# Tile norms, section sums, layer 1's scores and the first routing of a two-layer decoder trunk in another order, on one core

## The chip, the core and the metric

The kernel runs on one core of a Trainium2 chip. The metric is the device time of one execution in microseconds (us). The version before takes 1516.17 us in the median of three runs (1515.65 to 1516.95).

## What is computed

The reference is a two-layer decoder trunk on 256 tokens of width 1024, float32 in and out. Each layer turns a conditioning vector into six sections of 1024 values (shift, scale and gate of the mixer, then of the feed-forward part), normalizes the rows, runs a hybrid mixer, and adds a feed-forward part: a dense SwiGLU in layer 0, the top two of eight experts in layer 1.

```
mod = (silu(c) @ ada_w[l] + ada_b[l])          # sections 6l .. 6l+5: sh1, sc1, g1, sh2, sc2, g2
h = rmsnorm(x, norm_mix_w[l]) * (1 + sc1) + sh1
x = x + g1 * hybrid_mixer(h, ...)              # conv | HGRN2 recurrence | chunked gMLP, then @ w_o
h = rmsnorm(x, norm_ffn_w[l]) * (1 + sc2) + sh2
ffn = swiglu(h, w1, w3, w2)                    if l == 0
ffn = sum of gates[e] * swiglu_e(h), e in top-2 of softmax(h @ router_w + router_b)   if l == 1
x = x + g2 * ffn
out = rmsnorm(x, final_norm_w)
```

The recurrence of the HGRN2 branch is computed here as masked scores on nine levels (block sizes 1, 2, 4, ... 128 tokens), each a set of small matmuls whose result Vector keeps under a mask.

## The kernel before

The tokens are two tiles of 128 (tt = 0 and 1). The weights, 474 MB in all, are loaded once in pieces of 128x1024 into a ring of 11 buffers (`raw`). ScalarE copies each piece rounded (its high part), Vector subtracts to get the low part (`split`, a ring of six), and TensorE multiplies in three passes (high by high, low by high, high by low). `s_lo` counts the low parts, `s_used` the pieces that TensorE is done with. Each engine's program is written out by hand in order, and semaphores join them. PSUM has two rings with an order fixed by tables: single banks `psU` (`unit_plan`) and pairs of banks `psA` (`event_plan`); `open_unit` and `open_event` wait until the bank's last reader is done.

Four places matter here.

**Tile norms.** The last product before a norm (w_o in a mixer, w2 in the dense part) ends with four held pieces, so that tile 0 is complete before tile 1. In `norm_tiles` Vector adds each half row to the residual (`add_rows`), ScalarE squares (`tile_square`) and takes the root (`tile_root`), Vector scales the rows (`tile_rows`), TensorE transposes the tile (`turn_tile`), and ScalarE scales and shifts the eight transposed chunks out of PSUM (`tile_high`, one activation for each) and writes them in pairs, rounded, to `hS`. Vector subtracts for the low part (`tile_low`). Then `rows_by_tiles` multiplies the next weight: three pieces on tile 0, the transposes of tile 1, the fourth piece, and then four pieces on tile 1. n = 0 is the norm before the dense part, n = 1 that before layer 1's mixer, n = 2 the router's.

**Section sums.** Vector accumulates a section's product with the conditioning vector over eight pieces (`product`), and TensorE sums over the partitions against a column of ones: `ada_sum` makes eight columns of one PSUM bank, which `modulate` reads; `row_sum` makes a row. Sections 3 and 4 of layer 0 feed n = 0, sections 7 and 6 feed n = 1. Section 11 is summed too at the end of the dense part.

**Scores.** `level` makes the scores of one level on TensorE, `keep_scores` keeps them, `prepare` makes the next level's operands. `sgu_mix` (spatial gating) takes the next pair of banks after level 8, and so waits until level 7's scores are kept; `attend` waits for level 8's.

**Routing.** `logits` of both tiles, Vector's top two, a rank of each token among those of its expert (a matmul with a triangle of ones), a selection matrix, and `gather`, which multiplies the tokens by it. Then a loop over the experts' items begins; it takes half of the time.

## Time and profile before

| | |
|---|---|
| median of three runs | 1516.17 us |
| the profiled execution, its own time | 1515.74 us |
| span of its trace | 1513.9 us |
| TensorE busy | 1484.2 us (98%) |
| TensorE weight loads | 1260.1 us (83%) |
| Vector busy | 1300.1 us (86%) |
| ScalarE busy | 961.2 us (63%) |
| mean granted TensorE clock | 0.993 |

The time of an execution is the span plus about 1.8 us around it. Busy time of TensorE (PE) counts pipelined matmuls; PEld is its weight loads, DVE is Vector, ACT is ScalarE. A float32 matmul that isn't in the rounded format stands in the trace as two records: `ada_sum` has 8 matmuls and 16 records. The granted clock is 1.00 at 2.4 GHz and 0.50 at 1.2 GHz.

### The profile page before, as it was taken

The numbers are of one execution on the slowest core, as the hardware profiler recorded it, in microseconds if no ns is written. First come the engines' busy times: TensorE is split into PE (matmuls) and PEld (weight loads), VectorE is DVE, ScalarE is ACT, GpSimd is POOL, SyncE is SP. The second block draws the span as 40 slices with busy tenths as digits, with TensorE's granted clock in tenths as the row PEclk, the third lists the DMA queues.
The fourth block names the chain that finished last, engine by engine and source line by source line (L and its number), as shares of the span: only waits on it lengthen the run. The fifth ranks groups of instructions, "written<-read, shape, count | busy, mean of one in ns | idle before, by whom it ended". The sixth has DMA issues, their size and how long they took to land. (4 is left out here: it accounts for less than half of the span.)

```text
span 1513.9 us, 22427 instructions
## 1 busy us (share of the span) xinstructions
PE 1484.2 (98%) x7543; PEld 1260.1 (83%) x7543; DVE 1300.1 (86%) x1508; ACT 961.2 (63%) x1120; POOL 30.0 (2%) x50
## 2 busy tenths in 40 slices
PE   8999999999999999999899999999999999999997
PEld 7999888788887998888788888888888888888886
DVE  7999797687665798797799999999999999999998
ACT  3636445644435544444397887887878878788785
POOL 0000000000000000000010000000000000000100
PEclk9999999999999999999899999999999999999999
DMA  9956497599994745588299999999999999999993
GB/s 349 342 172 237 142 336 273 177 342 352 354 328 144 250 140 195 208 313 291 92 363 396 410 393 400 380 370 411 359 390 379 375 409 360 395 369 384 410 393 138
DMA packets 196979, 473.91 MB, mean 313 GB/s; under 512 B 16252, under 2 KB 64564, under 8 KB 196916
## 3 DMA queue, kind: packets, MB, share of 16 engines
q1 hardware_dynamic: 192288, 457.27, 82.1%
q0 software_dynamic: 4352, 15.73, 2.7%
q8 instruction: 36, 0.59, 0.2%
q14 instruction: 27, 0.22, 0.0%
q10 hardware_dynamic: 276, 0.09, 0.0%
HBM read 457.83 MB, written 15.21 MB: 312 GB/s over the span
## 5 line engine op out<-in xcount | busy, mean ns | idle before, releaser
L1339 ACT ACTIVATE split<-raw 128x1024 fp32r<-128x1024 f32 x750 | 780.5, 1061 | 281.7 <-PE psU L731 169.7
L2257 DVE TENSOR_TENSOR split<-raw,split 128x1024 fp32r<-128x1024 f32 x528 | 617.1, 1222 | 22.8 <-ACT split L1339 10.5
L731 PE MATMUL psU<-split,yS 128*128 128x512 f32 x2448 | 565.2, 390 | 0.2 <-DVE split L2257 0.2
L731 PEld LDWEIGHTS psU<-split,yS 128*128 128x128 f32 x2448 | 457.9, 188 | 95.3 <-DVE split L2257 0.8
L731 PE MATMUL psU<-split,hS 128*128 128x512 f32 (+1 forms) x1488 | 340.7, 387 | 1.4 <-DVE hS L1839 1.3
L731 PEld LDWEIGHTS psU<-split,hS 128*128 128x128 f32 x1488 | 273.4, 190 | 58.8 <-issue 5.1
L1656 DVE TENSOR_TENSOR split<-raw,split 128x1024 fp32r<-128x1024 f32 x222 | 264.1, 1219 | 42.8 <-ACT split L1339 41.9
L731 PE MATMUL psA<-split,hidE 128*128 128x512 f32 x1056 | 246.0, 392 | 0.0
L731 PEld LDWEIGHTS psA<-split,hidE 128*128 128x128 f32 x1056 | 196.5, 188 | 40.1
L731 PE MATMUL psU<-hS,split 128*128 128x256 f32 x1248 | 155.2, 285 | 0.1
L731 PEld LDWEIGHTS psU<-hS,split 128*128 128x128 f32 x1248 | 151.3, 192 | 1.3 <-issue 1.2
L1515 ACT ACTIVATE sig<-psU 128x512 f32<-128x512 f32 x24 | 13.0, 596 | 73.4 <-PE psU L731 73.4
L731 PE MATMUL psA<-split,hid_hi 128*128 128x512 f32 x176 | 55.2, 395 | 0.0
L1742 DVE SCALAR_TENSOR_TENSOR adacc<-raw,cact,adacc 128x1024 f32<-128x1024 f32 x42 | 53.8, 1281 | 1.1
L2438 DVE TENSOR_TENSOR hidE<-psA,hidE 128x512 fp32r<-128x512 f32 (+1 forms) x48 | 29.5, 643 | 14.4 <-ACT hidE L1339 14.4
L731 PEld LDWEIGHTS psA<-split,hid_hi 128*128 128x128 f32 x176 | 32.6, 188 | 6.9 <-issue 0.5
L1339 ACT ACTIVATE hidE<-psA 128x512 fp32r<-128x512 f32 (+1 forms) x48 | 25.3, 560 | 18.6 <-PE psA L1238 18.6
L2431 DVE TENSOR_TENSOR sig<-sig,psU 128x512 f32<-128x512 f32 (+1 forms) x48 | 29.3, 639 | 6.6 <-PE psU L731 6.6
L1597 ACT ACTIVATE sig<-psU 128x512 f32<-128x512 f32 (+1 forms) x48 | 25.3, 562 | 4.1 <-PE psU L731 4.1
L1339 ACT ACTIVATE work<-psU 128x512 f32<-128x512 f32 x18 | 10.4, 598 | 25.4 <-PE psU L731 20.6
L731 PE MATMUL psA<-split,hid 128*128 128x512 f32 x64 | 25.0, 390 | 0.0
L1238 PEld LDWEIGHTS psA<-ident,sig 128*128 128x128 f32 x176 | 21.3, 141 | 4.2
(287 smaller groups left out, 814.0 us busy)
## 6 DMA issues: line engine op xcount, KB each, us to landing
raw<-in_moe_w_dram SPq DMA_DIRECT2D x496, 512.0 KB, 5.9
raw<-in_w_in_dram SPq DMA_DIRECT2D x116, 512.0 KB, 6.0
raw<-in_ada_w_dram SPq DMA_DIRECT2D x96, 512.0 KB, 6.7
raw<-in_ffn_w_dram SPq DMA_DIRECT2D x66, 512.0 KB, 7.3
raw<-in_moe_w_dram SPq DMA_DIRECT2D x64, 256.0 KB, 6.2
raw<-in_w_o_dram SPq DMA_DIRECT2D x16, 512.0 KB, 5.9
token_rows<-sc SPq DMA_DIRECT2D x11, 512.0 KB, 10.7
raw<-in_w_br_a_dram SPq DMA_DIRECT2D x8, 512.0 KB, 6.7
```

What stands on the lines that cost most here:

```text
L731: return pe.matmul(o, a, b, start=start, stop=stop, skip_group_check=True)
L1238: last = pe.transpose(T_BANKS[g % 2][:, m * CAP:(m + 1) * CAP], sig[0:CAP, 2 + g % 2, m * P:(m + 1) * P], ident[0:CAP, 0:CAP])
L1339: return act.activation(o, i, ACT.Copy)
L1515: act.activation(sig[:, j, :], bank[:, :], ACT.Sigmoid).then_inc(s_uA, 1)
L1597: act.activation(sig[0:CAP, g % 2, 0:width], psU[3 if g == MIXED else g % 2][0:CAP, 0:width], ACT.Silu).then_inc(s_silu, 1)
L1656: TTN(split[:, n % SPL, 1, :], raw[:, SPLIT_POS[n] % RAW, :], split[:, n % SPL, 0, :].bitcast(F32), ALU.subtract).then_inc(s_lo, 1)
L1742: STT(acc, raw[:, pos % RAW, :], cact[:, k:k + 1], acc, ALU.mult, ALU.add).then_inc(s_afree, 1)
L2257: TTN(split[:, slot, 1, :], raw[:, (RAW0 + n) % RAW, :], split[:, slot, 0, :].bitcast(F32), ALU.subtract).then_inc(s_lo, 1)
L2431: TTN(sig[0:CAP, 2 + g % 2, 0:width], s, three, ALU.mult).then_inc(s_hrow, 1)
L2438: TTN(h_lo, T_BANKS[g % 2][:, 0:len(tiles) * CAP], h_hi.bitcast(F32), ALU.subtract).then_inc(s_hlo, 1)
```

## The change

- The three sums of `NORM_SUMS` (7, 6 and 11) no longer stand among the pieces of w2 but together between tile 0's and tile 1's held pieces. The sums of sections 3 and 4 in layer 0 stand between the two tiles' held pieces of w_o. Each of these sums now has 64 equal columns in place of one, eight times 64 filling a bank, of which `modulate` reads one.
- `turn_tile` of tile 0 comes two pieces earlier at n = 0, and one half row earlier at n = 1.
- In `tile_high` a chunk's activation no longer waits for the one before it; the copy of a pair comes one chunk late and waits only for its own two chunks.
- Vector's order in `norm_tiles` follows, with single chunk pairs between the residual's half rows.
- In layer 1 `keep_scores` of level 7 and the low parts of the next two pieces come before the last tap of the convolution.
- Tile 0 is ranked, selected and gathered on its own, while tile 1's logits and top two are made. The filling matmuls ahead of it are 2, not 4.

The diff, cut to its core:

```diff
-ROW_SUMS = [2, 5, 8, 9, 10]
...
-DOWN_SUM_AT = {2: 7, 3: 6, BANKWISE - 1: 11}
...
-FILL_LOGITS = 4
+FILL_LOGITS = 2
...
-        plan += [(("ada", 6 * l + s), "D") for s in (2, 3)]
-        plan += [((l, "merge", i), "merged") for i in range(2)] + [(("ada", 6 * l + 4), "D")]
+        plan += [(("ada", 6 * l + s), "D") for s in ((2, 3) if l else (2,))]
+        plan += [((l, "merge", i), "merged") for i in range(2)]
+        plan += [(("ada", 6 * l + s), "D") for s in ((4,) if l else (3, 4))]
...
-                    last = mm(bank[:, k:k + 1], acc[:, k * P:(k + 1) * P], ones[:, 0:1], True, True)
+                    last = mm(bank[:, k * WIDE:(k + 1) * WIDE], acc[:, k * P:(k + 1) * P], ones[:, 0:WIDE], True, True)
...
-            def section_sum(s):
-                row_sum(s) if s in ROW_SUMS else ada_sum(s)
...
-                        if (n, hh) == (2, 0):
-                            section_sum(6 * l + 3)
+                        if (l, n, hh) == (1, 2, 0):
+                            row_sum(9)
...
                         banks = [open_unit((l, "y" + b, 2 * hh + tt)) for tt in range(TT)]
...
-                        section_sum(6 * l + 2)
+                        row_sum(6 * l + 2)
...
                     if n == 1:
...
-                section_sum(6 * l + 4)
+                if l:
+                    row_sum(10)
                 for hh, q in WO_PIECES[HELD:]:
                     pe.wait_ge(s_ml, 4 * l + q + 1)
                     ws.append(next_split())
...
+                if l == 0:
+                    ada_sum(3)
+                    ada_sum(4)
...
                     rows_piece(wo[hh], q, ws[n], 1).then_inc(s_used, 1)
-                    if n == 2:
+                    if n == 2 * l:
...
-                    elif f in DOWN_SUM_AT:
-                        ada_sum(DOWN_SUM_AT[f])
...
-                                if f == NF - 2:
-                                    turn_tile(1, 0)
...
+                        if (tt, hh) == (0, 1):
+                            for s in NORM_SUMS:
+                                ada_sum(s)
+                        if (tt, hh) == (1, 0):
+                            turn_tile(1, 0)
...
-            def logits(tt):
...
-                for k in range(KD):
+            def logits(tt, ks=range(KD)):
...
+                for k in ks:
...
-                last.then_inc(s_unit, 1)
+                if ks[-1] == KD - 1:
+                    last.then_inc(s_unit, 1)
...
-            logits(1)
-            bank = open_unit("rank")
+            logits(1, range(4))
+            rank = open_unit("rank")
...
-            mm(bank[:, 0:NE], tri[:, :], route[:, 0, 0:NE], True, True)
-            mm(bank[:, NE:3 * NE], ones[:, :], route[:, 0:1, 0:NE].to_broadcast([P, 2, NE]), True, False)
-            mm(bank[:, NE:2 * NE], tri[:, :], route[:, 0, NE:2 * NE], False, True)
-            mm(bank[:, 2 * NE:3 * NE], ones[:, :], route[:, 0, NE:2 * NE], False, True).then_inc(s_unit, 1)
...
-            def gather(banks):
...
-                for m in range(KD):
-                    for tt in range(TT):
-                        last = mm(banks[m // 4][:, (m % 4) * CAP:(m % 4 + 1) * CAP], htok[:, tt, m * P:(m + 1) * P],
-                                  sel[:, 0, tt, :], tt == 0, tt == 1)
-                    if m % 4 == 3:
+            mm(rank[:, 0:NE], tri[:, :], route[:, 0, 0:NE], True, True)
+            mm(rank[:, NE:3 * NE], ones[:, :], route[:, 0:1, 0:NE].to_broadcast([P, 2, NE]), True, False).then_inc(s_rank, 1)
+            logits(1, range(4, KD))
...
+            def gather(banks, tt, ms):
...
+                pe.wait_ge(s_sel, tt + 1)
+                for m in ms:
+                    last = mm(banks[m // 4][:, (m % 4) * CAP:(m % 4 + 1) * CAP], htok[:, tt, m * P:(m + 1) * P],
+                              sel[:, 0, tt, :], tt == 0 and m % 4 == 0, tt == 1)
+                    if tt and m % 4 == 3:
...
-            pe.wait_ge(s_sel, 1)
-            gather(open_event("gather0"))
+            banks = open_event("gather0")
+            gather(banks, 0, range(6))
+            pe.wait_ge(s_rt, 2)
+            mm(rank[:, NE:2 * NE], tri[:, :], route[:, 0, NE:2 * NE], False, True)
+            mm(rank[:, 2 * NE:3 * NE], ones[:, :], route[:, 0, NE:2 * NE], False, True).then_inc(s_unit, 1)
+            gather(banks, 0, range(6, KD))
+            gather(banks, 1, range(KD))
...
+                first = step[0]
...
+                def pair_high(j):
+                    if j < 3:
+                        act.wait_ge(s_a, first + 2 * j + 2)
+                    else:
+                        act.wait_ge(s_eA, emptied(EVENTS, at, "A"))
+                    copy(hS[:, 0, 2 * j:2 * j + 2, tt * P:(tt + 1) * P],
+                         xn[tt][:, 2 * j * P:2 * (j + 1) * P].rearrange("p (a b) -> p a b", a=2)).then_inc(s_th, 1)
...
-                        act.wait_ge(s_eA, emptied(EVENTS, at, "A"))
...
-                        link(ins)
-                    if k % 2:
-                        copy(hS[:, 0, k - 1:k + 1, tt * P:(tt + 1) * P],
-                             xn[tt][:, (k - 1) * P:(k + 1) * P].rearrange("p (a b) -> p a b", a=2)).then_inc(s_th, 1)
+                        ins.then_inc(s_a, 1)
+                        step[0] += 1
+                    if k % 2 == 0 and k:
+                        pair_high(k // 2 - 1)
+                pair_high(3)
...
                 tile_root(n, 0)
+                if n == 0:
+                    high_parts(held + 7)
+                tile_high(n, 0)
...
-                tile_high(n, 0)
...
-                TTN(dst, bank[:, 0:KD], vecs[:, ADA_B + 8 * s:ADA_B + 8 * s + 8],
+                TTN(dst, bank[:, :].rearrange("p (k r) -> p k r", r=WIDE)[:, :, 0], vecs[:, ADA_B + 8 * s:ADA_B + 8 * s + 8],
...
                 tile_base(n, 0)
+                if n:
+                    modulate(7)
+                    modulate(6)
...
+                for s in ((11,) if n else (3, 4)):
+                    modulate(s)
+                if n == 0:
+                    low_parts(held + 7)
+                tile_low(n, 0, range(1))
...
+                tile_low(n, 0, range(1, 3))
+                add_rows(n, 1, 1, row)
+                tile_low(n, 0, range(3, 4))
...
-                tile_low(n, 0, range(2))
-                add_rows(n, 1, 1, row)
-                tile_low(n, 0, range(2, 4))
...
                 keep_scores(l, 6)
                 prepare(l, 8)
                 lows_beside((l, "i", 1))
+                if l:
+                    keep_scores(l, 7)
+                    lows_beside((l, "u", 0))
...
-                    elif j:
-                        lows_beside((l, "u", 0))
-                    keep_scores(l, 7 + j)
+                    if j or l == 0:
+                        keep_scores(l, 7 + j)
...
-                            else:
-                                modulate(3)
...
-                    modulate(4)
...
-                if f in (6, 7):
-                    modulate(NORM_SUMS[f - 6])
...
-            modulate(DOWN_ADA[0])
...
+                of = slice(tt * NE, (tt + 1) * NE)
...
-                TTN(route[:, LG, tt * NE:(tt + 1) * NE], bank[:, 0:NE], rtb[:, :], ALU.add).then_inc(s_uD, 1)
+                TTN(route[:, LG, of], bank[:, 0:NE], rtb[:, :], ALU.add).then_inc(s_uD, 1)
...
-                link(dve.max(mx8[:, tt, :], route[:, LG, tt * NE:(tt + 1) * NE]))
-                settle()
-                link(dve.max_index(ix8[:, tt, :], mx8[:, tt, :], route[:, LG, tt * NE:(tt + 1) * NE]))
-                settle()
-                link(dve.tensor_copy(route[:, IDX, tt * NE:(tt + 1) * NE], ix8[:, tt, :]))
+                link(dve.max(mx8[:, tt, :], route[:, LG, of]))
+                settle()
+                link(dve.max_index(ix8[:, tt, :], mx8[:, tt, :], route[:, LG, of]))
+                settle()
+                link(dve.tensor_copy(route[:, IDX, of], ix8[:, tt, :]))
...
-                    link(TS(route[:, row, tt * NE:(tt + 1) * NE], iota8,
-                            route[:, IDX, tt * NE + k:tt * NE + k + 1], None, ALU.is_equal))
-            TTN(cur[:, 0:2], mx8[:, :, 0], mx8[:, :, 1], ALU.subtract).then_inc(s_prob, 1)
-            settle()
-            TTN(route[:, SEL, :], route[:, ONE, :], route[:, TWO, :], ALU.add).then_inc(s_rt, 1)
-            dve.wait_ge(s_rt, 1)
-            bank = unit("rank")
-            link(TTN(route[:, POS, :], bank[:, 0:2 * NE], route[:, SEL, :], ALU.mult))
-            dve.tensor_copy(route[:, CNT, 0:NE], bank[:, 2 * NE:3 * NE]).then_inc(s_uD, 1)
-            settle()
-            for tt in range(TT):
+                    link(TS(route[:, row, of], iota8, route[:, IDX, tt * NE + k:tt * NE + k + 1], None, ALU.is_equal))
+                settle()
+                TTN(route[:, SEL, of], route[:, ONE, of], route[:, TWO, of], ALU.add).then_inc(s_rt, 1)
+                dve.wait_ge(s_rt, tt + 1)
+                if tt:
+                    bank = ready("rank")
+                else:
+                    dve.wait_ge(s_rank, 1)
+                    bank = psU[UNIT_AT["rank"] % 4]
+                link(TTN(route[:, POS, of], bank[:, of], route[:, SEL, of], ALU.mult))
+                settle()
...
-                ins = TS(sel[:, 0, tt, :], slots[:, :], route[:, POS, tt * NE:tt * NE + 1], None, ALU.is_equal)
-                if tt == 0:
-                    link(ins)
-            ins.then_inc(s_sel, 1)
+                TS(sel[:, 0, tt, :], slots[:, :], route[:, POS, tt * NE:tt * NE + 1], None, ALU.is_equal).then_inc(s_sel, 1)
+            dve.tensor_copy(route[:, CNT, 0:NE], bank[:, 2 * NE:3 * NE]).then_inc(s_uD, 1)
+            TTN(cur[:, 0:2], mx8[:, :, 0], mx8[:, :, 1], ALU.subtract).then_inc(s_prob, 1)
...
```

The order of instructions, with the wait of each in brackets. First TensorE's program at n = 0, in layer 0's w_o and the dense part's first pieces (`psU<-split,hS` are the pieces, `psA<-ident,merged` the transposes of a tile, `psA<-ones,...` the section sums), as a piece of the difference:

```order
 L837 MATMUL psA<-ident,merged 128x128 x8
-L731 MATMUL psU<-split,hS 128x512 x24
-L731 MATMUL psA<-ones,work 128x1 x8
-L731 MATMUL psU<-split,hS 128x512 x42
+L731 MATMUL psU<-split,hS 128x512 x48
+L731 MATMUL psA<-ones,adacc 128x64 x8
+L731 MATMUL psA<-ones,work 128x64 x8
+L731 MATMUL psU<-split,hS 128x512 x6
 L799 MATMUL psA<-ident,merged 128x128 x8
-L731 MATMUL psU<-split,hS 128x512 x24
+L731 MATMUL psU<-split,hS 128x512 x36
 L799 MATMUL psA<-ident,merged 128x128 x8
```

Both sums now stand between the 24 held matmuls of tile 0 and those of tile 1, and tile 0's transposes have three held pieces and three pieces of tile 0 behind them where they had one and three.

Vector's program in layer 1 around the last scores, before (`sc<-...` keeps scores, `split` rows make low parts, `work<-work,vecs` is the tap, `work<-psA,vecs,sgub` reads the spatial gating):

```order
L1955 TENSOR_TENSOR work<-work 128x4x128
L2078 SCALAR_TENSOR_TENSOR work<-work,vecs 128x254 [waits dve_step]
L2078 SCALAR_TENSOR_TENSOR work<-work,vecs 128x254 x3
L2091 TENSOR_TENSOR work<-work 128x1024 [waits dve_step]
L1996 COPY_PREDICATED sc<-masks,psA 128x512 [waits dve_event_emptied,event_ready]
L1996 COPY_PREDICATED sc<-masks_back,psA 128x4x128
L1656 TENSOR_TENSOR split<-raw,split 128x1024 [waits act_high_parts] x2
L1992 COPY sc<-psA 128x512 [waits dve_event_emptied,event_ready]
```

and now:

```order
L1981 TENSOR_TENSOR work<-work 128x4x128
L2022 COPY_PREDICATED sc<-masks,psA 128x512 [waits dve_event_emptied,event_ready]
L2022 COPY_PREDICATED sc<-masks_back,psA 128x4x128
L1674 TENSOR_TENSOR split<-raw,split 128x1024 [waits act_high_parts] x2
L2104 SCALAR_TENSOR_TENSOR work<-work,vecs 128x254 [waits dve_step]
L2104 SCALAR_TENSOR_TENSOR work<-work,vecs 128x254 x3
L2120 TENSOR_TENSOR work<-work 128x1024 [waits dve_step]
L2018 COPY sc<-psA 128x512 [waits dve_event_emptied,event_ready]
```

The level-7 scores and the two low parts moved ahead of the five instructions of the convolution.

TensorE's program from the second logits to the gather, before (`rtw,merged` logits, `route` the rank, `sc,work` the gather):

```order
L731 MATMUL psU<-rtw,merged 128x64 [waits router_first_chunks_ready]
L731 MATMUL psU<-rtw,merged 128x64 x3
L731 MATMUL psU<-rtw,merged 128x64 [waits act_event_emptied]
L731 MATMUL psU<-rtw,merged 128x64 x3
L731 MATMUL psU<-route,tri 128x8 [waits routing_ready,dve_unit_emptied]
L731 MATMUL psU<-route,ones 128x16
L731 MATMUL psU<-route,tri 128x8
L731 MATMUL psU<-route,ones 128x8
L731 MATMUL psA<-sc,work 128x128 [waits act_event_emptied,selection_ready]
L731 MATMUL psA<-sc,work 128x128 x15
```

and now:

```order
L731 MATMUL psU<-rtw,merged 128x64 x3
L731 MATMUL psU<-route,tri 128x8 [waits selected_experts_ready,dve_unit_emptied]
L731 MATMUL psU<-route,ones 128x16
L731 MATMUL psU<-rtw,merged 128x64 [waits act_event_emptied]
L731 MATMUL psU<-rtw,merged 128x64 x3
L731 MATMUL psA<-sc,work 128x128 [waits selection_ready,act_event_emptied]
L731 MATMUL psA<-sc,work 128x128 x5
L731 MATMUL psU<-route,tri 128x8 [waits selected_experts_ready]
L731 MATMUL psU<-route,ones 128x8
L731 MATMUL psA<-sc,work 128x128 [waits selection_ready]
L731 MATMUL psA<-sc,work 128x128
L731 MATMUL psA<-sc,work 128x128 [waits selection_ready]
```

Tile 0's rank stands between two halves of the logits, and half of the gather no longer waits for tile 1.

## Rows read from the trace of the kernel before

**Rows 1.** The page's first part, busy time of TensorE: us, share, instructions.
```profile
PE 1484.2 (98%) x7543; PEld 1260.1 (83%) x7543; DVE 1300.1 (86%) x1508; ACT 961.2 (63%) x1120; POOL 30.0 (2%) x50
```
**Rows 2.** Waits of TensorE, longest first: us in total, times, longest.
```profile
PE psA L799 <- DVE split L1656: 5.1, 2, 2.5
...
PE psA L731 <- DVE sc L1996: 3.0, 1, 3.0
```
**Rows 3.** Windows of TensorE: length, PE busy and count, granted clock, DMA.
```profile
283.80:287.20 3.40, 3.15 (x12) 0.54 0.53 152
484.90:488.30 3.40, 3.40 (x10) 0.50 0.51 155
580.70:584.00 3.30, 3.30 (x18) 0.51 0.00 0
734.00:737.50 3.50, 3.10 (x12) 0.51 0.00 0
747.80:754.70 6.90, 6.05 (x29) 0.51 0.01 2
```
**Rows 4.** Timeline, n = 0: start, length, engine, line, count, [idle before].
```profile
264.53 9.84 PE L731 MATMUL psU<-split,hS 128*128 128x512 f32 x42
...
280.10 0.61 ACT L1385 ACTIVATE sig<-xs 128x512 f32<-128x512 f32 x1
...
282.77 1.22 DVE L1656 TENSOR_TENSOR split<-raw,split 128x1024 fp32r<-128x1024 f32 x1
...
284.05 1.97 PE L799 MATMUL psA<-ident,merged 128*128 128x128 f32 x8 [2.54 <-DVE split L1656]
```
**Rows 5.** Timeline, n = 1, TensorE.
```profile
463.67 0.72 PE L731 MATMUL psA<-split,hid_hi 128*128 128x512 f32 x2
...
476.74 4.58 PE L731 MATMUL psU<-split,hS 128*128 128x512 f32 x18 [0.98 <-DVE hS L1839]
...
483.86 1.09 PE L799 MATMUL psA<-ident,merged 128*128 128x128 f32 x8 [2.55 <-DVE split L1656]
...
484.71 8.68 PE L731 MATMUL psU<-split,hS 128*128 128x512 f32 x30
```
**Rows 6.** Timeline, layer 1's last scores.
```profile
576.04 1.65 DVE L2078 SCALAR_TENSOR_TENSOR work<-work,vecs 128x254 f32<-128x254 f32 x4
...
577.72 1.23 DVE L2091 TENSOR_TENSOR work<-work 128x1024 f32<-128x1024 f32 x1
...
580.32 3.60 PE L731 MATMUL psA<-wT,merged 128*128 128x128 f32 x16 [3.00 <-DVE sc L1996]
...
601.40 3.35 DVE L2139 RECIPROCAL work<-work 128x512 f32<-128x512 f32 x1 [1.82 <-ACT work L1357]
```
**Rows 7.** Timeline, routing.
```profile
745.83 0.17 DVE L2304 TENSOR_TENSOR route<-psU,rtb 128x8 f32<-128x8 f32 x1 [1.94 <-PE psU L731]
...
747.44 0.36 PE L731 MATMUL psU<-route,tri 128*128 128x8 f32 x2 [1.64 <-DVE route L2317]
...
749.85 6.07 PE L731 MATMUL psA<-sc,work 128*128 128x128 f32 x32 [0.85 <-DVE sc L2326]
...
755.68 14.63 PE L731 MATMUL psU<-split,yS 128*128 128x512 f32 x63
```
**Rows 8.** Timeline: a one-column sum, 64-column logits, small matmuls at 1.00.
```profile
461.97 1.84 PE L731 MATMUL psU<-ones,adacc 128*128 128x1 f32 x16
...
589.57 2.84 PE L731 MATMUL psA<-sc,work 128*128 128x128 f32 x24
...
738.17 1.89 PE L731 MATMUL psU<-rtw,merged 128*128 128x64 f32 x16
```
**Rows 9.** Timeline, ScalarE, the first chunks of tile 0 at n = 0.
```profile
274.92 0.95 ACT L1410 ACTIVATE merged<-psA,mod,wm 128x128 f32<-128x128 f32 x2 [1.15 <-PE psA L799]
...
275.90 0.42 ACT L1339 ACTIVATE hS<-merged 128x256 fp32r<-128x256 f32 x1
...
276.23 0.93 ACT L1410 ACTIVATE merged<-psA,mod,wm 128x128 f32<-128x128 f32 x2
```

3 lines of the change are left out of this document (2 added, 1 removed).

## The prediction

> **What bounds the kernel now.** I read the page's busy shares first: TensorE is busy for 1484.2 of 1513.9 us, and 29.7 us are idle [rows 1]. Some 1450 us are matmuls one behind the other that the change doesn't touch, so only TensorE's idle stretches and its slow ones can give anything. TensorE's waits come next: twice 2.5 us for a low part at a tile's transposes, and 3.0 us for Vector's kept scores [rows 2]. Then the windows, read for the granted clock: it is at 2.4 GHz everywhere but in five stretches, at 1.2 GHz for about 3.4 us in four of them and for 6.9 us in the last [rows 3]. Each stretch begins at or just behind an idle one of TensorE [rows 4 to 7]. A wait therefore costs more than its length. The change lies at four of the five places (284, 485, 581 and 748 us). At the fifth, 734 us, the transposes of the router's first tile keep their order, and I leave it as it is.
>
> **Part A, the norm before the dense part.** Count from the first held matmul of tile 0 (264.53 us). Before, tile 1's transposes begin 19.5 us later, at 284.05 [rows 4]. The two sums stood ahead of that point, 1.84 us each (16 records of one column [rows 8]), which makes 23.2 us for the same work. Now: 24 matmuls of 0.234 us (9.84 / 42 [rows 4]) are 5.6; the two sums at 1.89 (as the 64-column logits [rows 8]) bring 9.4; six held matmuls 10.8; tile 0's transposes, 1.09 [rows 5], 11.9; 18 held matmuls 16.1; 18 on tile 0's new rows 20.3. TensorE is then ready for tile 1. What is late next is tile 1's own chain. Its last half row exists at 16.1, and Vector's product and sum with it take about 1.5, to 17.7. Before, the turn came 3.95 us after the first of two squares (280.10 to 284.05 [rows 4]); now only the second is left, 0.6 less, so the turn is at about 21.1. That needs ScalarE to be done with tile 0's chunks by then. Before, a pair takes 1.31 us (274.92 to 276.23) because each activation waits for the one ahead; one without a wait starts 0.09 before the end of the last (276.23 against 275.90 + 0.42) [rows 9]. Two activations of 0.36 and a copy of 0.33 make 1.05 a pair and 4.4 for the tile: from 12.0 to 16.4, in time. The wait shrinks from 2.5 to about 0.9, and the turn comes 2.1 earlier.
>
> Behind the turn the clock matters. Before, it is low for 3.4 us, and the transposes with the next six matmuls take 3.65 (284.05 to 287.7, by the count in [rows 3]); at the high level they take 1.09 + 1.40, plus some 0.35 until the first pair of tile 1 is written: 2.85. That gives 0.8 more. TensorE waited 0.98 us at 476.74 with the clock still up behind it [rows 5], so I expect none to fall at 0.9. A: 2.1 + 0.8 = 2.9.
>
> The Trainium skill, "ScalarE: Activation LUTs", section "What ACT_TABLE_LOAD costs", says that back-to-back activations overlap by about 93 ns and that each pointer operand adds about 93. The overlap agrees with the 0.09 of the row [rows 9]. By the page's figures a chunk with two pointers would take 479 ns less 93, an estimate of 0.39 in place of my 0.36, and the tile 0.2 us longer; as ScalarE is done 1.3 us ahead, the sum stays.
>
> **Part B, the norm before layer 1's mixer.** Count from 463.67, where tile 0's first half row begins. Before, the turn of tile 1 is at 20.2 (483.86), and the three sums stood ahead: 25.7. Now: two half rows of 12 matmuls 5.5; three sums 5.7, to 11.2; a half row 14.0; tile 0's transposes 15.1; the last half row 17.9; two pieces 20.7. The third piece needs a low part that Vector makes only after both of tile 1's half rows are added. In Vector's queue the first of these stands behind tile 0's first chunk pair (about 16.8), so: add to 18.2, two pairs 18.9, add 20.3, a pair 20.7, the low part of 1.22 [rows 4] 22.0. TensorE waits 1.3, and is at 23.4 ready for tile 1. That chain (root, reciprocal, two scalings, another low part of 1.22) ends at 24.7: a second wait of 1.3. Before, the waits were 0.98 and 2.55 [rows 5]; gain to the turn 1.0. The 30 matmuls behind it took 8.68 us at the low and then the high clock against 7.0 [rows 5]; less a new wait of 0.35, and with the transposes' own share, 0.9 more if the clock stays up. B: 1.9. It is the weakest term, since a whole piece isn't enough to part the two waits.
>
> **Part C, layer 1's scores.** Vector was at the last tap from 576.04 (1.65), then the product (1.23), and only then kept level 7, for which TensorE waited 3.00 us [rows 6]. Now keeping (1.35) begins at 576.0 and ends at 577.4, when TensorE has just made level 8 (577.3): the wait is about 0.15, a gain of 2.85. The clock stood at 0.51 for 3.3 us of work [rows 3]; at full it is some 1.35 shorter (16 records of 0.118 [rows 8] in place of 3.2 us). C: 4.2. What the moved work now delays: the product of the convolution ends at 582.7 in place of 579.0, for which ScalarE waits with a copy that TensorE needs only at the gates, over 15 us later. Level 8's scores are kept at 583.4, and `attend` comes at 585.5. Two reciprocals of 3.35 us on Vector are next in line (601.40); before these it waited 1.82 us for ScalarE and TensorE [rows 6], so they move up with TensorE. The two moved low parts cost nothing: they were due behind.
>
> **Part D, routing.** Two filling matmuls less let the transposes of tile 1 begin 0.5 earlier, when its rows are ready. From there: 1.3 until the first chunks are copied, four logits 0.95, tile 0's rank 0.6, four logits 0.95: 3.8. Vector needs 1.5 from there to tile 1's selected experts (745.83 to 747.3 [rows 7]); TensorE meanwhile gathers six chunks of tile 0, 12 records, 1.4. A rank of 0.7 brings 6.0, two chunks 6.5, and tile 1's selection comes 0.85 after the rank (the wait before 749.85 [rows 7]), at 6.9. Its 16 records take 1.9, to 8.8; Vector's list of items and the first low tokens hold the loop until 9.6. Before, it was 755.68 - 742.51 = 13.2. That is 3.6 + 0.5; I take 3.5 for all of it, as three more hand-overs between engines stand in the path at 0.1 to 0.3 each. This contains idle time of 0.85 + 1.64 [rows 7] and the half clock of 6.9 us [rows 3].
>
> **Wider sums and the rest.** A sum of 64 columns costs what one of a single column does, 118 against 115 ns a record [rows 8]: five sums, 0.2 us more. Taking section 3's sum out of the third branch and the others out of the pieces of w2 only brings TensorE forward there, where no wait is recorded. No DMA is moved.
>
> **The sum.** 2.9 + 1.9 + 4.2 + 3.5 - 0.2 = 12.3 us. The profiled execution took 1515.74 (span 1513.9 and 1.8 around it), so it would take 1503.4. The median of the runs is 0.43 above it: 1516.17 - 12.3 = 1503.9 us.
>
> Bounds of the terms: A from 1.2 (a clock that falls after all) to 4.1; B from 0 to 3.5; C from 2.8 (wait gone, low clock kept) to 4.6; D from 1.5 to 5.5.
>
> **Rivals.** First, the clock falls all the same. For it: B has two waits of 1.3 around 1.4 us of work, and in the routing 1.64 idle behind thin matmuls were enough (747.44, low from 747.8 [rows 3, 7]); the three sums in a row are thin for 5.7 us, longer than any such run in the trace of before. Against: 0.98 did nothing [rows 5], and logits of the same width ran at 1.00 from 738.17 [rows 8]. Each fall costs about 1.5; two falls, or one and a longer chain in B, give 1503.9 + 2.7 = 1506.6 us.
>
> Second, C is given back. If Vector, busy for 86% of the span [rows 1], can't follow TensorE by 4.2 us into the branches (the reciprocals, 6.7 us together, stand between two low parts there), the wait returns behind 601 us. Against it: Vector waited there itself. Price: 1503.9 + 4.2 = 1508.1.
>
> Third, nothing arrives: the expert loop is bound by its weights' transfers, and TensorE, reaching it 12 us earlier, would wait there. Against it, the DMA share is 0.00 to 0.01 in the windows before the loop [rows 3], since all 11 buffers are full. It would give 1516 us.
>
> Fourth, slower. The mechanism is the clock at the moved sums: were thin matmuls, alone on TensorE, to pull it down at A and B and keep it down through the pieces behind, each microsecond there would cost half of itself. All five stretches of before hold 20.5 us [rows 3]. The gain from idle time alone is about 7 us, so the kernel gets slower once the low clock lasts over 14 us more than before; 22 us more, as much of the dense part's first group, give 1516.2 + 4 = 1520.
>
> **How the numbers follow.** I give the forecast 0.55, and on its better side, with B's or D's chain shorter than I counted, 0.08; the clock's fall 0.22, C given back 0.07, nothing 0.05, slower 0.03. What a measurement of this kernel can tell from no change is 0.2%, 3.0 us; the first four cases are beyond it. So faster 0.92, the same 0.05, slower 0.03. The range goes from 1500.5, below the forecast by D's upper bound and part of B's, to 1508.5, which holds the clock's fall and C given back.
>
> **What the profile after would show.** The clock at 1.00 around the two tile norms and the spatial gating; one stretch of low clock left before the loop, at about 725 us, and none behind it. TensorE's waits at tile 1's transposes at 0.9 (n = 0) and 1.3 (n = 1), with another of 1.3 one piece ahead of it at n = 1; the wait for kept scores under 0.3. ScalarE's chunk pairs 1.05 us apart. The loop starting some 12 us earlier, at 743 to 744. What would make the prediction wrong: low clock behind the three sums or between B's two waits, and a new wait of TensorE for a low part in the branches.

## The result and the profile after

The changed kernel takes 1501.6 us (median of 4 runs, 1500.76 to 1501.92); the kernel before takes 1515.95 beside it (4 runs, 1515.65 to 1516.95). The ratio is 0.9903, 95% interval 0.9886 to 0.9920. The gain is 14.35 us where 12.3 were forecast; 1501.6 lies in the range of 1500.5 to 1508.5. The profiled execution of the changed kernel took 1501.51, its span is 1499.7.

First the page's busy times, then TensorE's waits, as in [rows 1, 2]:

```profile
PE 1477.1 (98%) x7539; PEld 1253.3 (84%) x7539; DVE 1300.3 (87%) x1510; ACT 958.2 (64%) x1120; POOL 31.1 (2%) x50
```
```profile
PE psA L799 <- DVE work L2300: 3.2, 2, 3.0
...
PE psA L799 <- DVE split L1674: 2.2, 2, 1.2
...
PE psU L731 <- DVE split L1674: 1.2, 2, 1.0
```

TensorE idles 1499.7 - 1477.1 = 22.6 us in place of 29.7, and is busy for 7.1 us less. Of its busy time, two filling matmuls (0.43 each by the run with 13 fillers below) are gone; most of the rest is work that ran at 1.2 GHz before. So about half of the gain is idle time, and nearly as much is the clock. The wait for kept scores has left the head of the list.

The windows of the changed kernel at the places of [rows 3], and at the moved sums (length, PE busy and count, granted clock, DMA share, GB/s):

```profile
266.70:270.20 3.50, 3.50 (x34) 1.00 0.98 362
283.00:286.40 3.40, 3.13 (x15) 1.00 0.54 154
460.95:466.20 5.25, 5.25 (x49) 1.00 0.02 8
479.30:482.70 3.40, 3.14 (x17) 1.00 0.58 183
573.60:577.00 3.40, 3.40 (x31) 1.00 0.00 0
725.00:728.50 3.50, 3.50 (x12) 0.51 0.00 0
731.00:737.90 6.90, 6.49 (x50) 1.00 0.01 2
```

The low stretches of [rows 3] at the two norms, at the spatial gating and in the routing are gone. One is left, at 725 us, as the prediction said. The timeline at the norm ahead of the dense part, answering to [rows 4], then at the one ahead of layer 1's mixer, to [rows 5]:

```profile
266.71 1.89 PE L731 MATMUL psA<-ones,adacc 128*128 128x64 f32 x16
268.43 1.95 PE L731 MATMUL psA<-ones,work 128*128 128x64 f32 x16
...
282.07 1.09 PE L799 MATMUL psA<-ident,merged 128*128 128x128 f32 x8 [1.19 <-DVE split L1674]
```
```profile
460.95 3.68 PE L731 MATMUL psU<-ones,merged 128*128 128x64 f32 x32
464.47 1.95 PE L731 MATMUL psU<-ones,adacc 128*128 128x64 f32 x16
...
476.59 1.65 PE L731 MATMUL psU<-split,hS 128*128 128x512 f32 x6 [1.01 <-DVE split L1674]
479.29 1.09 PE L799 MATMUL psA<-ident,merged 128*128 128x128 f32 x8 [1.05 <-DVE split L1674]
```

ScalarE's chunks of tile 0 at the second norm, to compare with [rows 9]. Two chunks begin at 471.15 and the next two at 472.15, 1.00 us apart where it was 1.31; between them stands the copy of a pair:

```profile
471.15 0.81 ACT L1426 ACTIVATE merged<-psA,mod,wm 128x128 f32<-128x128 f32 x2
471.84 0.43 ACT L1346 ACTIVATE hS<-merged 128x256 fp32r<-128x256 f32 x1
472.15 0.82 ACT L1426 ACTIVATE merged<-psA,mod,wm 128x128 f32<-128x128 f32 x2
```

Layer 1's last scores, to [rows 6]: the sixteen matmuls of the spatial gating wait 0.16 us and take 2.02 in place of 3.60; Vector reaches the reciprocal without a wait.

```profile
571.87 2.02 PE L731 MATMUL psA<-wT,merged 128*128 128x128 f32 x16 [0.16 <-DVE sc L2022]
...
591.60 3.35 DVE L2167 RECIPROCAL work<-work 128x512 f32<-128x512 f32 x1
```

Routing, to [rows 7]: tile 0's rank stands between two halves of tile 1's logits, and the loop starts at 742.01.

```profile
724.32 1.56 PE L799 MATMUL psA<-ident,work 128*128 128x128 f32 x8 [3.05 <-DVE work L2300]
...
732.17 1.23 PE L799 MATMUL psA<-ident,work 128*128 128x128 f32 x8 [0.17 <-DVE work L2300]
733.49 1.10 PE L731 MATMUL psU<-rtw,merged 128*128 128x64 f32 x8
734.43 0.34 PE L731 MATMUL psU<-route,tri 128*128 128x8 f32 x2
...
742.01 20.25 PE L731 MATMUL psU<-split,yS 128*128 128x512 f32 x88 [1.22 <-DVE yS L2431]
```

For a split by parts I compared where the same work begins in the two traces. The anchors of before that are not in the rows above, and those of after:

```profile
182.23 1.02 PE L731 MATMUL psU<-split,hS 128*128 128x512 f32 x2
...
306.76 1.03 PE L1068 MATMUL psA<-ident,sig 128*128 128x128 f32 x8
...
529.56 0.61 PE L731 MATMUL psA<-work 128*128 128x128 f32 x4
...
605.46 0.86 PE L731 MATMUL psU<-split,hS 128*128 128x512 f32 x3
```
```profile
182.50 0.79 PE L731 MATMUL psU<-split,hS 128*128 128x512 f32 x1
...
304.00 1.03 PE L1069 MATMUL psA<-ident,sig 128*128 128x128 f32 x8
...
523.94 1.06 PE L731 MATMUL psA<-work 128*128 128x128 f32 x8
...
595.37 10.84 PE L731 MATMUL psU<-split,hS 128*128 128x512 f32 x47
```

| Part | Work that stands earlier behind it | Seen | Forecast |
|---|---|---|---|
| A, norm n = 0 | 306.76 to 304.00, plus 0.27 that the execution was late at 182 us | 3.03 | 2.9, less 0.1 for wider sums |
| B, norm n = 1 | 529.56 to 523.94 is 5.62, less 2.76 | 2.86 | 1.9, less 0.1 |
| C, layer 1's scores | 605.46 to 595.37 is 10.09, less 5.62 | 4.47 | 4.2 |
| D, routing | 755.68 to 742.01 is 13.67, less 10.09 | 3.58 | 3.5 |

Inside the loop another 0.52 us come by 806.20 (there 792.01, 14.19 earlier), and nothing more to its end. First before, then after:

```profile
783.87 7.05 PE L731 MATMUL psU<-split,yS 128*128 128x512 f32 x30
...
806.20 1.04 PE L1238 MATMUL psA<-ident,sig 128*128 128x128 f32 x8
```
```profile
770.15 22.02 PE L731 MATMUL psU<-split,yS 128*128 128x512 f32 x96
...
792.01 1.04 PE L1245 MATMUL psA<-ident,sig 128*128 128x128 f32 x8
```

No edit stands there, and yet this is no accident of two executions. Between these two places lie 22.33 us before and 21.86 after. All five profiles of kernels with the old routing have 22.31 to 22.36 us there, and all nine with the new one 21.86 to 22.04. So the half microsecond belongs to the routing's part, which brings 4.1 us in all. In the trace of before, ScalarE waits 0.60 us there for a piece's transfer and TensorE 0.17 for the low part made from it; why the routing's order settles this, no run shows.

### The profile page after: what moved, and what is told of

The parts are those of the page before. It is cut to its first block, busy times and chain, and to the rows that moved or that the text cites. A ratio compares the mean times of both kernels' runs of the same rounds, so it can differ in the third digit from the quotient of the medians.

```text
span 1499.7 us, 22422 instructions
## 1 busy us (share of the span) xinstructions
PE 1477.1 (98%) x7539; PEld 1253.3 (84%) x7539; DVE 1300.3 (87%) x1510; ACT 958.2 (64%) x1120; POOL 31.1 (2%) x50
## 4 chain that ended last, share of the span: by engine, by line
PE 89%; DVE 8%; issue 1%; ACT 1%; DMA 1%; POOL 0%; DVEq 0%; ACTq 0%; POOLq 0%
PE psU L731 64%; PE psA L731 22%; DVE split L1674 2%; PE psA L1245 1%; DVE sc L2022 1%; DMA raw<-in_ada_w_dram 1%; PE psU L1201 0%; DVE work L1993 0%; DVE work L1992 0%; DVE work L2003 0%; PE psA L799 0%; PE psA L1069 0%; DVE xs L1832 0%; DVE sig L1822 0%; DVE adacc L1901 0%
```

## The experiments

Low clock is summed over windows of 0.5 us between 240 and 800 us; by it the kernel before has 20.5 us and the changed one 3.4.

**Each part alone, on the kernel before.** Three kernels, each with its hunks of the diff and nothing else. The scores' kernel has this one:

```
 lows_beside((l, "i", 1))
+if l:
+    keep_scores(l, 7)
+    lows_beside((l, "u", 0))
 tap(2)
```

The routing's kernel has `FILL_LOGITS`, `logits(tt, ks)`, `gather(banks, tt, ms)` and Vector's loop over the two tiles; the norms' kernel has the moved and widened sums, the chunk writes and Vector's order in `norm_tiles`, of which the core is:

```
-                    if n == 2:
-                        turn_tile(2 * l, 0)
+                    if n == 2 * l:
+                        turn_tile(2 * l, 0)
```

> The kernel before with one part of the change alone: in layer 1 the scores of level 7 are kept, and two low parts made, ahead of the last tap and the product of the convolution. Theory (terms add up): by the two traces the work behind the spatial gating stands 4.46 us earlier against the work ahead of it, so this kernel takes 4.2 to 4.5 us less than before. TensorE's wait there falls from 3.00 to under 0.3 us (2.85 less), and the clock stays at 2.4 GHz behind it (1.4 to 1.6 less). Rival (only the wait): the clock falls all the same, 2.9 us less. Rival (given back): without the earlier parts' gain Vector stands otherwise at the two reciprocals, and part of it returns as a wait in the branches: 0 to 2 us less.

> The kernel before with the routing part alone: tile 0 ranked and gathered beside tile 1, two filling matmuls in place of four. Theory: 3.6 us at the start of the expert loop and 0.5 more somewhere behind it by the traces, so 3.6 to 4.1 us less than before, with the low clock of 747.8 to 754.7 us gone and TensorE's first loop matmul still waiting about 1.2 us for Vector's low part of the second half of the tokens. Rival: the half microsecond behind the loop's start was an accident of the two profiled executions: 3.5 us less.

> The kernel before with the two tile norms' part alone (the sums moved and 64 columns wide, chunk writes without waits, Vector's order). Theory: 3.07 us at the norm ahead of the dense part and 2.82 us at that ahead of layer 1's mixer by the two traces, 5.9 us less than before; the waits for low parts are 1.2 us once and 1.0 us twice, the clock stays up. Rival (the terms of the prediction were right and the rest an accident): 4.8 us less. Rival (the gain is only carried if Vector is relieved by the other order of layer 1's scores): under 4 us less, with a longer wait for the kept scores than 3.0 us.

| Kernel | Median us | Ratio to before (1515.64), 95% | Gain by the ratio | Low clock |
|---|---|---|---|---|
| scores alone | 1511.9 | 0.9975 (0.9966 to 0.9985) | 3.8 | 13.7 |
| routing alone | 1511.9 | 0.9972 (0.9960 to 0.9983) | 4.2 | 13.7 |
| norms alone | 1510.68 | 0.9966 (0.9954 to 0.9979) | 5.2 | 17.1 |

Scores alone: 3.8, below the 4.2 to 4.5 of the theory but with them inside its interval of 2.3 to 5.2, which excludes "given back" (0 to 2). "Only the wait" (2.9) is not excluded by this time, but by its profile: the gating's sixteen matmuls take 2.02 us there behind a wait of 0.17, and from the transposes ahead of them to the first piece behind the scores pass 24.82 us (575.77 to 600.59) in place of 29.29 (576.17 to 605.46 before), which is 4.47 less, as in the changed kernel. Routing alone agrees with the theory's 3.6 to 4.1; its interval (2.6 to 6.1) doesn't exclude the rival's 3.5, but its profile has the half microsecond in the loop too (21.90 us in place of 22.33), so that wasn't an accident. Norms alone agrees with 5.9; its interval (3.2 to 7.0) excludes neither rival. Its profile has the theory's waits, 1.18 once, 1.01 and 1.04, with no low clock behind them, and a wait for the kept scores of 2.99, no longer than before. The three gains sum to 13.2, the change as a whole gives 14.7 by its own ratio; with intervals of about 1.5 us each, the parts can't be told from additive.

One thing in these profiles explains part of the spread. With the kept-scores wait still in place, the norms' kernel shows this, where the kernel before had half of it [rows 3, 6]:

```profile
575.21 3.75 PE L730 MATMUL psA<-wT,merged 128*128 128x128 f32 x16 [2.99 <-DVE sc L2016]
578.62 6.90 PE L730 MATMUL psU<-hS,split 128*128 128x256 f32 x48
```
```profile
574.20:581.00 6.80, 5.79 (x28) 0.52 0.01 1
```

The same wait of 3.0 us brought 3.4 us of low clock in one execution and 6.8 in another (6.8 also in the profile of the routing's kernel). And the wait of 2.5 at the first norm, which nobody had touched there, brought none in the profile of the scores' kernel.

**Sums one column wide.** In the changed kernel:

```
-last = mm(bank[:, k * WIDE:(k + 1) * WIDE], ..., ones[:, 0:WIDE], True, True)
+last = mm(bank[:, k * WIDE:k * WIDE + 1], ..., ones[:, 0:1], True, True)
```

> The changed kernel with its five moved sums (two at the norm ahead of the dense part, three in a row at that ahead of layer 1's mixer) one column wide as before, in place of 64. Theory of the prediction: width costs nothing (118 against 115 ns a record), so 0.2 us less than the changed kernel if the clock is not touched. Rival: 1.9 and 5.6 us of one-column matmuls alone on TensorE, with waits of 1.0 to 1.2 us close behind, let the granted clock fall to 1.2 GHz behind the two norms' sums: 1.5 us more for one such stretch, 3 us more for two.

1508.67 us, ratio 0.9952 (0.9935 to 0.9969): 7.1 us slower than the changed kernel, over twice the rival's price, and the theory of the prediction is dead. Two of the four runs took 1507.1 and 1507.3 us, the other two 1510.0 and 1510.2; the profile is of one of the latter. Windows, then timeline:

```profile
267.40:270.20 2.80, 2.80 (x26) 0.95 0.96 349
270.20:276.00 5.80, 5.80 (x22) 0.50 0.31 120
464.90:468.00 3.10, 3.10 (x30) 0.98 0.03 11
468.00:477.50 9.50, 9.50 (x34) 0.50 0.00 0
```
```profile
464.88 4.06 PE L731 MATMUL psU<-ones,merged 128*128 128x1 f32 x32
468.80 3.55 PE L731 MATMUL psU<-ones,adacc 128*128 128x1 f32 x16
```

TensorE was never idle there, and yet the clock fell to 1.2 GHz in the middle of the sums, for 6.8 us at the first norm and 10.2 at the second: 17 us of low clock, at half speed 8.5 us of work time less what idle time took up. With 64 columns the windows at 266.70 and 460.95 above, over the same sums, stand at 1.00. Widening the sums is not a part of the change that costs 0.2 us; without it the clock takes back more than both norms' parts bring (5.2 us by time, 5.9 by the traces).

**Chunk writes that wait again**, in the changed kernel; the copy of a pair stands right behind its two chunks again, too:

```
-ins.then_inc(s_a, 1)
-step[0] += 1
+link(ins)
```

> The changed kernel with ScalarE's chunk writes each waiting for the one ahead again (a pair in 1.31 us in place of 1.00), all else as changed. Theory of the prediction: tile 0's chunks take 1.2 us longer, and at the norm ahead of the dense part ScalarE was done 1.3 us before it was needed, so nothing is lost there; at the one ahead of layer 1's mixer Vector's low part stands behind the third pair, which comes 0.6 to 0.9 later, so its waits grow by that: 0.5 to 1.0 us more than the changed kernel. Rival: each norm's last chain (root, chunks, first pair) carries it twice and a wait passes from 1.0 to about 1.9 us, with a fall of the clock behind: 2.5 to 4 us more. Rival (of no weight): the same time.

1503.09 us, ratio 0.9917 (0.9901 to 0.9934): 1.5 more, half a microsecond above the theory's 0.5 to 1.0. The wait at the first norm is the same as without the edit, 1.23 us against 1.19, as expected. At the second the place is the one that was named, with a wait of 1.74 in place of 1.01:

```profile
478.52 1.66 PE L731 MATMUL psU<-split,hS 128*128 128x512 f32 x6 [1.74 <-DVE split L1665]
```

The clock stays at 1.00 behind it. Of the 1.5 us 0.73 are thus found; the rest is within what the comparison can tell.

**One norm put back at a time**, in the changed kernel: n = 1 (sums among w2's pieces, tile 0's transposes one piece before the end), then n = 0 (sums in the third branch and before the held pieces, transposes behind the third held piece). Vector's and ScalarE's order at that norm goes back with them. In both kernels the sums stay 64 wide and the chunk writes without waits. On TensorE the two edits are these:

```
+elif f in DOWN_SUM_AT:
+    ada_sum(DOWN_SUM_AT[f])
...
-if (tt, hh) == (0, 1):
-    for s in NORM_SUMS:
-        ada_sum(s)
```
```
-if l:
-    row_sum(10)
+row_sum(10) if l else ada_sum(4)
...
-if l == 0:
-    ada_sum(3)
-    ada_sum(4)
...
-if n == 2 * l:
+if n == 2:
```

> The changed kernel with the norm ahead of layer 1's mixer alone put back: its three sums (still 64 columns wide) among the pieces of w2, tile 0's transposes one piece before the end, Vector's and ScalarE's order there as before. Theory: the wait of 2.55 us at tile 1's transposes is back in place of one of 1.05 us and costs 1.5 us for itself; the clock behind it falls in some executions for 3.4 us (it did in the kernel before, not in the one with the routing alone), 1.3 to 1.5 more: so 1.5 us more than the changed kernel without a fall, 2.8 with one. Prediction's own figure for this part: 1.9. Rival: under 1.0 us more, the part being carried by the other edits.

> The changed kernel with the norm ahead of the dense part alone put back: section 3's sum in the third branch, section 4's before the held pieces (both 64 columns wide), tile 0's transposes behind the third held piece, Vector's and ScalarE's order there as before; the chunk writes stay without waits. Theory: the shorter chunks take 0.8 us off the wait at tile 1's transposes, as they did at the other norm, where undoing brought 1.70 in place of 2.55 us: so a wait of 1.7 where the changed kernel has 1.2, two sums back to places where TensorE had them anyway; 0.6 to 1.2 us more than the changed kernel if the clock stays up, 2.2 if it falls once. Rival (prediction's own figure for this part): 2.9 us more.

1502.71 us for n = 1 (ratio 0.9915, 0.9898 to 0.9931) and 1502.89 for n = 0 (0.9911, 0.9895 to 0.9926): 1.1 and 1.3 more than the changed kernel. The intervals of these ratios and of the chunks' one overlap with the changed kernel's; but none of the twelve runs (1502.03 and up) is as fast as its slowest (1501.92). Both profiles have the same wait at tile 1's transposes, first n = 1, then n = 0:

```profile
480.00 1.09 PE L800 MATMUL psA<-ident,merged 128*128 128x128 f32 x8 [1.70 <-DVE split L1672]
```
```profile
283.18 1.09 PE L799 MATMUL psA<-ident,merged 128*128 128x128 f32 x8 [1.68 <-DVE split L1671]
```

The first theory missed: it had 2.55 us come back at n = 1 and at least 1.5 us of time, but only 1.70 did, since the chunks without waits shorten that chain by themselves by 0.85. The second, made from this, has its wait (1.68 for 1.7) and lies 0.1 under the measured time; its rival's 2.9 didn't come. And at 1.7 us of idle time the transposes behind take 1.09, which is the full clock. So a gain of 2.9 at either norm is made by two edits that overlap: each alone takes the wait from 2.55 under 2, and with it most of the clock's loss is gone. Put back one by one, the reordering (sums, transposes, Vector's order) is worth 1.1 and 1.3 and the chunk writes 1.5, 3.9 together, of the 5.2 (by the traces 5.9) that all bring. (Both profiles have 6.8 us of low clock at 724 where that of the changed kernel has 3.4; the place was not touched.)

**Fillers in the wait for kept scores**, on the kernel before. `stream(free_unit(), 13)` makes 13 matmuls into a single bank that is free, and nobody reads their result. That wait keeps its length, only TensorE isn't idle in it.

```
+if l:
+    stream(free_unit(), 13)     # 6 in the second kernel
 pe.wait_ge(s_uD, emptied(UNITS, UNIT_AT[(l, "v", 1)], "D"))
```

> The kernel before with 13 filling matmuls (256 columns, 0.215 us each, 2.8 us in all) on TensorE where it waits 3.00 us for the kept scores in layer 1; nothing else is changed, and no wait is shortened. Theory (half of part C is the clock): the work behind begins no earlier, but no low clock is left at that place, so 1.4 us less than before where before has one stretch of 3.4 us of low clock there, up to 3 us less where it has two. Rival (the wait is all, the clock is a matter of chance): the same time as before, or 0.1 to 0.3 us more because the fillers overrun the wait, and a low stretch at 580 us in the profile.

> The kernel before with 6 filling matmuls (2.6 us) in the wait of 3.00 us for the kept scores; 13 of them took 5.78 us, pushed the work behind by 2.8, and yet the kernel took the same time as before. Theory (behind an idle stretch of this length the clock falls, for one stretch of 3.4 us in some executions and for two in others): the wait's end stays where it is, no low clock at that place, 1.4 to 2.8 us less than before, 1513.0 to 1514.3. Rival (the clock does not matter there): the time of before.

With 13 I had mistaken one record for one matmul: a filler is two records, 0.43 us, and the thirteen took 5.78 in a wait of 3.00:

```profile
576.68 5.78 PE L737 MATMUL psU<-sgub,ones 128*128 128x256 f32 x26
```

That kernel took 1516.4 us, ratio 1.0002 (0.9993 to 1.0012): TensorE was given 2.8 us of work beyond the wait, and the time stayed. The theory's 1.4 to 3 us less didn't come, and the number is the rival's; but its low stretch at 580 us isn't there. The two traces show why the time stayed. Counted from the transposes ahead of the wait (576.17 before, 575.68 here), the gating's matmuls begin 2.46 us later (at 582.29 in place of 580.32), and of these 1.71 are won back by the first piece behind the scores (605.46 and 605.72): work at 2.4 GHz in place of 1.2. The 0.75 that are left lie within the interval. With 6, in 2.76 us, the work behind begins at its old distance, and the kernel takes 1513.91, ratio 0.9985 (0.9976 to 0.9994), 2.3 us less than before:

```profile
576.83 2.76 PE L737 MATMUL psU<-sgub,ones 128*128 128x256 f32 x12
579.99 2.02 PE L737 MATMUL psA<-wT,merged 128*128 128x128 f32 x16 [0.40 <-DVE sc L2004]
```
```profile
580.00:583.40 3.40, 3.40 (x29) 1.00 0.01 2
```

This settles the clock's share of C by itself: six matmuls whose result nobody reads give 0.9 to 3.6 us. The traces are finer. From the transposes ahead of the wait to the first piece behind the scores pass 29.29 us before, 27.66 with six fillers (575.84 to 603.50), 30.18 in the norms' kernel (571.07 to 601.25) with its low clock of 6.8 us. So the low clock behind this wait costs 1.6 us where it lasts 3.4, and 2.5 where it lasts 6.8, beside 3.0 for the wait. (The profile with six fillers also lacks the low stretch at n = 1, which the edit doesn't touch; so a part of the 2.3 may be chance.)

**Fillers ahead of the router's first tile**, in the changed kernel, in its last wait of 3.05 us.

```
 if n == 2 * l:
+    if l:
+        stream(free_unit(), 13)     # 6 in the second kernel
     turn_tile(2 * l, 0)
```

> The changed kernel with 13 filling matmuls (256 columns, 2.8 us) on TensorE in its last wait of 3.05 us, ahead of the transposes of the router's first tile. It is the one place in the changed kernel behind which the clock is low. Theory: the transposes and the six held matmuls behind them take 1.04 and 1.4 us in place of 1.56 and 2.91, the low stretch of 3.4 us is gone, and the loop starts 1.5 to 1.9 us earlier: 1.5 us less than the changed kernel, about 1500.0. Rival (the next thing is late): tile 1's row sums bind the transposes of tile 1 whatever TensorE's clock, and at most 0.3 us of it arrives. Rival: the low clock moves behind the next wait: no change.

> As the run with fillers ahead of the router's first tile, but with 6 in place of 13: the profile showed one of them to be two records, 0.43 us, so that 13 took 5.77 us in a wait of 3.05 and 6 take 2.6. Theory: from the transposes of the router's first tile to the loop that run took 15.97 us where the changed kernel takes 17.69; now they begin at their old time, so 1.7 us less than the changed kernel, 1499.9 us, and no low clock before the loop. Rival (what the long fill gained came from Vector being ahead, not from the clock): the low stretch returns or the next wait grows, and the time is that of the changed kernel, 1501.6 us.

With 13 (again 5.77 us, 2.7 too many) 1502.37 us, ratio 0.9913 (0.9896 to 0.9929), 0.8 more than the changed kernel where 1.5 less were expected; with 6 1500.27, ratio 0.9896 (0.9881 to 0.9911), 1.3 less than the changed kernel and 0.4 above the forecast of 1499.9. The runs of the last two overlap (1499.39 to 1501.07 against 1500.76 to 1501.92); what carries the reading is the profile of the kernel with 6. No window between 240 and 800 us is under 0.98 there, and the router's transposes take 1.23 us in place of 1.56:

```profile
724.14 1.23 PE L805 MATMUL psA<-ident,work 128*128 128x128 f32 x8 [0.45 <-DVE work L2308]
```

The loop starts 16.19 us behind these transposes (740.33) in place of 17.69, 1.5 us less.

**The count of items earlier**, on top of that: `nitem` is made ahead of the three lists and has a semaphore of its own.

```
+TS(nitem[:, :], total[:, src, 2 * NO - 1:2 * NO], float(NE), None, ALU.add).then_inc(s_count, 1)
 for r in range(REX):
     link(STT(picked[:, r, :], ...))
-link(TS(nitem[:, :], total[:, src, 2 * NO - 1:2 * NO], float(NE), None, ALU.add))
...
-pe.wait_ge(s_items, 1)
+pe.wait_ge(s_count, 1)
```

> The one before with one edit more: the number of expert items, which TensorE reads before the loop, is made ahead of the three lists of extra items and signalled by itself; in the changed kernel TensorE idles 1.2 us before the loop's first matmul, which starts 1.3 us behind the end of the item list. Theory: the count is there 0.9 us earlier, TensorE then starts when the tokens' first low part is there, 0.6 us earlier than now: 1499.3 us, the wait before the loop 0.6 us. Rival (the wait is for the low part and TensorE's own step into the loop): 0 to 0.1 us less, the same wait of 1.2 us.

1499.65 us, ratio 0.9892 (0.9877 to 0.9907), 0.6 less again; the wait before the loop shrinks from 1.22 to 0.67, as the theory said:

```profile
738.77 0.69 DVE L2440 TENSOR_TENSOR yS<-psA,yS 128x512 fp32r<-128x512 f32 x1
```
```profile
739.60 27.50 PE L738 MATMUL psU<-split,yS 128*128 128x512 f32 x120 [0.67 <-DVE yS L2440]
```

In the changed kernel the trace puts this wait down to the tokens' low part, whose write ended at 741.32, 0.7 ahead of TensorE's start; it was the count that TensorE reads. Now TensorE starts 0.14 us behind the end of that low part (738.77 + 0.69), and the low part is what binds. This is the fastest version here, 2.0 us below the changed kernel by the medians of two comparisons, each beside the kernel before.

## Why the prediction was right, and what in it was not

The likeliest case came true: the gain arrives at all four places, none is given back, and the one low stretch that was to be left is left. The four windows of low clock behind the changed places are gone; none of the rivals happened. Two of four terms (A and C) are within 0.3 us in the comparison of the traces; B and D came out 1.0 and 0.6 larger.

*Part A*: 3.0 for 2.9. The wait is 1.19 for "about 0.9". Tile 1's turn stands 1.98 us earlier (284.05 to 282.07), 2.25 with the 0.27 by which this execution was late, for 2.1; behind it 0.78 come, for 0.8. ScalarE was done in time; with waits in its chunks again, the wait there is the same (1.23 against 1.19). By the figures of the Trainium skill, "ScalarE: Activation LUTs", section "What ACT_TABLE_LOAD costs", a chunk would cost an estimated 0.39. Here the copy begins 0.69 us behind the start of two chunks (471.15 to 471.84), 0.35 each. The measurement decides for the row.

*Part B*, called the weakest term, is the most mis-sized one: 2.9 seen for 1.9. To tile 1's turn it is 1.8 (483.86 to 479.29 is 4.57, less 2.76) for 1.0. The waits are 1.01 and 1.05, not 1.3 and 1.3, which is 0.55. Most of the rest is that I priced each sum at its printed 1.84 to 1.89 us. A group's length contains 0.15 or so in which it overlaps the next group: from start to start a sum takes 1.72 (266.71 to 268.43), and three of them 5.28 (460.95 to 466.23), not 5.7. Behind the turn 1.05 come for 0.9, and the two waits with 1.4 us of work between them don't lower the clock. That the 0.9 fits is luck in part: the prediction's own terms, 8.68 less 7.0 less 0.35, make 1.3.

*Part C*: 4.5 for 4.2; the wait of 0.16 as forecast, no wait in front of the reciprocals. Of the 4.5, 2.8 are the wait and 1.6 the clock, the forecast's "some 1.35"; that the clock has this share is shown by the fillers, not only read from rows.

*Part D*: 3.6 for 3.5 up to the loop, and 0.5 more within it, which the prediction didn't have; 4.1 in all. The prediction's own count gave 3.6 + 0.5, and it took 3.5 to leave room for hand-overs. How much of D is idle time, clock or the two fillers less was not tried apart. The mark "a wait of 0.85 for tile 1's selection" is covered by tile 0's gathers; what ends the stretch is the count of items, which I had in the sum as "Vector's list of items and the first low tokens" without telling the two apart.

*Wider sums*, forecast -0.2 us, fails as a step though the sum wasn't hurt by it. The prediction weighed width by its price alone (118 against 115 ns a record), and set the clock at the moved sums under "slower" with a chance of 3 in 100, for 64 columns. At 64 that was right. For one column the fourth rival's mechanism exists, at 7.1 us: thin matmuls alone on TensorE do pull the clock down, without any idle time. The trace of before held a one-column sum at 1.00 [rows 8], but it was single, between pieces.

*The total*: 14.35 for 12.3. By the traces the parts sum to 14.5, 2.2 over the forecast: B gives 1.0 of it, D 0.6, C 0.3, A 0.1, and the 0.2 that wider sums were to cost is already within what was seen. Less the 0.27 at 182 us, the sum is 14.2, the difference of the two spans. How much of a part is clock depends on the execution. Over the 46 runs of the kernel before beside the experiments, the 18 with a mean granted clock of 0.992 have a mean of 1516.58 us, the 14 at 0.994 1515.54, and the 6 at 0.995 1513.98. Whether the change also narrowed this spread isn't shown: its four runs lie within 1.2 us, but so, within 1.3, do the four of the kernel before beside them.

What stays open: why the same wait is followed by no low stretch, one of 3.4 us or one of 6.8. The Trainium skill, "TensorE: Matmul & The Clock Gate", section "What's actually happening", says that the number of slow matmuls at a kernel's start differs from run to run of one kernel. No run here looks at a start; in the middle of this kernel the profiles show something like it. Behind the wait of 2.5 us at n = 0 the clock fell in four profiles of five, at n = 1 in two of five, and behind the waits of 3.0 at the scores (three profiles) and the router (eleven) in every one. Behind waits of 1.7 us at the norms it fell in none of three.

## What to carry to other kernels

Price an idle stretch of the bounding engine by what runs behind it as well: here 3.0 us of waiting at the scores cost 1.6 to 2.5 us more behind them, and a few matmuls into a free bank, counted so that they end just before the wait does, buy that part back where the wait itself can't be shortened. Before moving small matmuls together, look at what else is on TensorE there and try them wider: here one column in place of 64 cost 7.1 us with TensorE never idle. And price a group by start to start, not by its printed length.

## What the runs showed that I had not expected

- Five moved sums of one column cost 7.1 us more than the same of 64 columns; the granted clock fell within the sums (from about 270 and 468 us), with TensorE busy throughout.
- 2.8 us of useless work beyond a wait of 3.0 us left the time as it was (1.0002, 0.9993 to 1.0012); 1.7 of them came back by the clock behind.
- The order of the routing takes 0.45 us off a stretch inside the loop that no edit touches, in nine profiles of nine against five of five.
- A filling matmul of 256 columns in fp32 is two records, 0.43 us from start to start, and count and time in a timeline row are per record.
- TensorE's first matmul of the loop starts 1.3 us behind the item list's end (740.69 to 742.01) although the trace names another releaser, and the wait is 0.55 shorter when the count is signalled by itself.
